# Input projection as seven block products in place of eight, in two passes over half of k

## The chip, the core and the metric

The program runs on one core of a Trainium2 chip. The metric is the device time of one execution in microseconds. All times of single instructions below come from one profiled execution of the kernel.

## What is computed

One decoder layer with two gated branches. Cut to what the change touches:

```python
h, gate = modulate(xp, c_prompt, g_norm[l], w_ada[l], b_ada[l])      # (tokens, 2048)
(q_a, k_a, v_a, z_a, q_b, k_b, v_b, z_b, q_i, k_i, w_i, g_a, g_b) = jnp.split(h @ w_in, offs, axis=-1)
q_a = rope(q_a.reshape(B, T, N_QH_A, HEAD_DIM), pos)                # k_a, q_b, k_b, q_i, k_i alike
...
s = jnp.einsum('bthd,bsd->bths', q_i, k_i) * (IDX_DIM ** -0.5)      # index scores
scores = jnp.einsum('bths,bth->bts', jax.nn.relu(s), w_i)           # then the top 256 keys of a row
...
y = (sigmoid(g_a) * u_a + sigmoid(g_b) * u_b) @ w_out
```

All is in float32. There are 1024 prompt tokens and 64 sample tokens, 1088 columns in all, and 10052 columns of w_in.

## The kernel before

The kernel is written engine by engine, in raw instructions with semaphores; each engine runs its own list in the order in which it is written, and no planner moves anything. TensorE multiplies float32 as three products of rounded parts: w_hi x h_hi, w_hi x h_lo and w_lo x h_hi, where the remainder ("lo") is the raw value less its rounded part ("hi").

Activations stand transposed: h_hi and h_lo hold 16 k tiles of 128 rows by 1088 tokens. The projection goes through w_in in tiles of 128 columns. Three index tiles come first (first_products, third_products; leave_index turns them by the rotary angle on VectorE), then the index scores (index_scores on VectorE, relu on ScalarE), then 76 main tiles in products (N_MAIN 44 and N_GATE 32, the last two in last_products). For a main tile SP loads w_raw, 1 MB (load_tile), ScalarE rounds it (split_hi), VectorE subtracts (split_lo), and TensorE runs three token chunks (CHUNKS, 384, 352 and 352 columns), each 16 k x 3 matmuls into a bank of PSUM. A finished chunk leaves its bank through ScalarE with its activation function (leave_act) or, for q and k, through VectorE with the rotary turn (leave_rotated: swapped halves times the sine into rot_b, values times the cosine into rot_a, the sum into col). GpSimd does no arithmetic in this stretch; it issues the stores of col to the scratch array proj. The table RUNS says which tiles leave how, and in which of them VectorE does rounds of the top 8 search (pick_round: MAX8 and MATCH_REPLACE8 on a row of 1088 scores, eight rounds a tile in 28 tiles).

While tiles of the gate columns run, conditioned and folded put in the matmuls of the adaLN gate (16 groups). After the last tile the attention begins (pe_attention and its likes): it loads keys and values back from proj into k_t and v_t, over the memory of h_hi and h_lo.

Main lines: matmuls L293 to L295, split_hi L279, split_lo L284, leave_act L372, leave_rotated L388 to L403, index scores L2258 to L2269, top 8 L2216 and L2218, h_lo L2544, the later weights' remainder u_lo L1944, GpSimd's o_raw L1836 and L1839.

## Time and profile before

| | us |
|---|---|
| median of 3 runs | 3147.2 |
| lowest, highest | 3143.88, 3154.12 |
| span of the profiled execution, first to last instruction | 3146.0 |
| of it: projection of the 76 main tiles | 1823.1 |
| of it: attention, merge and output | 1107.3 |

The profile has TensorE's matmuls (PE) and weight loads (PEld), VectorE (DVE), ScalarE (ACT), GpSimd (POOL) and SP's DMA issues (SPq). "Busy" is the time in which an engine executes. A matmul's time is longer than the distance to the next one, since they overlap; the distance between starts is what counts. "Idle before" names what an engine waited for.

### The profile page before, as it was taken

How to read it: one execution, taken by the hardware profiler on the slowest of the kernel's cores; microseconds unless marked ns; L12 is line 12 of the kernel's file. 1: busy time of each engine (PE TensorE's matmuls, PEld its weight loads, DVE VectorE, ACT ScalarE, POOL GpSimd, SP SyncE). 2: the span in 40 equal slices, each digit the busy share in tenths (PEclk: the TensorE clock that was granted, in tenths of full speed). 3: DMA queues.
4: the chain of work that ended last, by engine and by line, in shares of the span. 5: the costliest groups of instructions: out<-in, count | busy, mean ns of one | idle time of the engine just before them, and what ended most of it. 6: DMA issues, size and time to landing. Idle time of an engine off the chain costs nothing. (4 is left out here: it accounts for less than half of the span.)

```text
span 3146.0 us, 50501 instructions
## 1 busy us (share of the span) xinstructions
PE 3054.7 (97%) x19803; PEld 2881.1 (92%) x19811; DVE 1693.4 (54%) x2463; ACT 749.9 (24%) x1173; POOL 266.7 (8%) x516
## 2 busy tenths in 40 slices
PE   5989999999999999999999999999999999999998
PEld 4869999999999999999999999988876897998986
DVE  4573786200786355555455554566654544654755
ACT  5240000011000111211111111165433323333333
POOL 3100000000000000000000000042224101010000
PEclk8999999999999999999999999999999999999999
DMA  9832222222222222333233232565269774683672
GB/s 350 282 114 70 75 74 61 82 61 61 82 75 61 94 63 75 105 93 102 75 95 109 81 102 75 181 198 147 85 188 312 215 269 158 194 269 127 207 237 98
DMA packets 452309, 425.08 MB, mean 135 GB/s; under 512 B 20628, under 2 KB 393620, under 8 KB 449108
## 3 DMA queue, kind: packets, MB, share of 16 engines
q1 hardware_dynamic: 428998, 343.06, 36.8%
q0 software_dynamic: 22048, 78.45, 6.7%
q10 hardware_dynamic: 1152, 2.13, 0.2%
q8 instruction: 65, 1.06, 0.1%
q14 instruction: 46, 0.38, 0.0%
HBM read 348.79 MB, written 76.88 MB: 135 GB/s over the span
## 5 line engine op out<-in xcount | busy, mean ns | idle before, releaser
L293 PE MATMUL banks<-h_hi,w_hi 128*128 128x352 f32 (+1 forms) x3552 | 1162.5, 327 | 0.0
L295 PE MATMUL banks<-h_hi,w_lo 128*128 128x352 f32 (+1 forms) x3552 | 1158.3, 326 | 0.0
L294 PE MATMUL banks<-h_lo,w_hi 128*128 128x352 f32 (+1 forms) x3552 | 1157.4, 326 | 0.0
L293 PEld LDWEIGHTS banks<-h_hi,w_hi 128*128 128x128 f32 x3552 | 666.8, 188 | 3.1 <-issue 3.0
L294 PEld LDWEIGHTS banks<-h_lo,w_hi 128*128 128x128 f32 x3552 | 669.2, 188 | 0.0
L295 PEld LDWEIGHTS banks<-h_hi,w_lo 128*128 128x128 f32 x3552 | 666.2, 188 | 0.0
L284 DVE TENSOR_TENSOR w_lo<-w_raw,w_hi 128x2048 fp32r<-128x2048 f32 x77 | 175.4, 2278 | 657.3 <-ACT w_hi L279 519.6
L372 ACT ACTIVATE col<-banks 128x384 f32<-128x384 f32 x150 | 71.2, 474 | 1023.6 <-PE banks L295 984.0
L1944 DVE TENSOR_TENSOR u_lo<-u_raw,u_hi 128x1536 fp32r<-128x1536 f32 (+1 forms) x96 | 196.4, 2046 | 200.4 <-ACT u_hi L1858 200.0
L2216 DVE MAX8 best<-work 128x8 f32<-128x1088 f32 x224 | 289.1, 1291 | 10.0
L2218 DVE MATCH_REPLACE8 work<-best,work 128x1088 f32<-128x1088 f32 x224 | 285.9, 1276 | 0.0
L279 ACT CAST w_hi<-w_raw 128x2048 fp32r<-128x2048 f32 x77 | 146.0, 1896 | 570.7 <-PE banks L295 552.8
L1858 ACT CAST u_hi<-u_raw 128x1536 fp32r<-128x1536 f32 (+1 forms) x96 | 162.8, 1696 | 410.8 <-PE banks L2202 231.1
L2200 PE MATMUL banks<-u_hi,m_hi 128*128 128x512 f32 x512 | 200.0, 391 | 5.8 <-DVE u_lo L1944 5.8
L2201 PE MATMUL banks<-u_hi,m_lo 128*128 128x512 f32 x512 | 199.7, 390 | 0.0
L2202 PE MATMUL banks<-u_lo,m_hi 128*128 128x512 f32 x512 | 199.7, 390 | 0.0
L2136 PE MATMUL banks<-o_hi,u_hi 128*128 128x384 f32 (+1 forms) x576 | 188.1, 327 | 1.0 <-DVE u_lo L1944 0.9
L2386 POOL DMA_DIRECT2D scratch_proj<-col x76 | 40.4, 531 | 1749.5 <-ACT col L372 1125.6
L2138 PE MATMUL banks<-o_hi,u_lo 128*128 128x384 f32 (+1 forms) x576 | 187.7, 326 | 0.0
L2137 PE MATMUL banks<-o_lo,u_hi 128*128 128x384 f32 (+1 forms) x576 | 187.6, 326 | 0.0
L388 DVE TENSOR_TENSOR rot_b<-banks,rot_sin 64x384 f32<-64x384 f32 (+1 forms) x156 | 83.2, 533 | 176.5 <-PE banks L295 174.6
L2200 PEld LDWEIGHTS banks<-u_hi,m_hi 128*128 128x128 f32 x512 | 96.5, 188 | 26.2 <-DVE u_lo L1944 6.2
(313 smaller groups left out, 3432.0 us busy)
## 6 DMA issues: line engine op xcount, KB each, us to landing
w_raw<-in_w_in SPq DMA_DIRECT2D x76, 1024.0 KB, 5.5
u_raw<-in_w_out SPq DMA_DIRECT2D x96, 512.0 KB, 5.0
scratch_proj<-col POOLq DMA_DIRECT2D x76, 544.0 KB, 3.0
ada_w<-in_w_ada SPq DMA_DIRECT2D x16, 2048.0 KB, 13.9
u_raw<-in_w_pb SPq DMA_DIRECT2D x48, 512.0 KB, 4.9
...
```

The costliest lines, as they stand in the source:

```text
L293: nc.tensor.matmul(dst, w_hi[:, par, k, 0:width], h_hi[:, k, a:b], start=(k == 0), stop=False)
L294: nc.tensor.matmul(dst, w_hi[:, par, k, 0:width], h_lo[:, k, a:b], start=False, stop=False)
L295: mm = nc.tensor.matmul(dst, w_lo[:, par, k, 0:width], h_hi[:, k, a:b], start=False, stop=(k == KT - 1))
L1944: nc.vector.tensor_tensor(u_lo[u % 2][:, 0:ks, :], u_raw[:, u, 0:ks, :], u_hi[u % 2][:, 0:ks, :], ALU.subtract).then_inc(u_lo_set, 1)
L2136: nc.tensor.matmul(dst, u_hi[par][:, k, :], hi[:, k, 0:n], start=(k == (whole or ks)[0]), stop=False)
L2137: nc.tensor.matmul(dst, u_hi[par][:, k, :], lo[:, k, 0:n], start=False, stop=False)
L2138: mm = nc.tensor.matmul(dst, u_lo[par][:, k, :], hi[:, k, 0:n], start=False, stop=(k == (whole or ks)[-1]))
L2200: nc.tensor.matmul(dst, high, hi[:, x, :], start=first, stop=False)
L2201: nc.tensor.matmul(dst, low, hi[:, x, :], start=False, stop=False)
L2202: mm = nc.tensor.matmul(dst, high, lo[:, x, :], start=False, stop=last)
L2216: nc.vector.max(best8[:], work[:])
L2218: nc.vector.match_replace(work[:], best8[:], work[:], TAKEN)
```

## The change

The 76 main tiles become 38 pairs, and each pair a product of 2 by 2 blocks: tokens in two halves of HT = 544 columns, a pair's two tiles, and k in two sets. Seven block products (P1 to P7, Strassen's form in Winograd's order) take the place of eight. They need sums of blocks on either side. On the side of h these are S1 to S4, made once for a pass; on the side of the weights four sums a step (t1 to t4, weight_sums on GpSimd). Each of the seven weight blocks is split into hi (ScalarE) and lo (VectorE five, GpSimd two). Since h, its sums and all hi and lo parts don't fit at once, the whole runs in two passes over half of k: steps 0 to 37 with k tiles 0 to 7, steps 38 to 75 with k tiles 8 to 15. In the first pass the half sums are stored to proj; in the second they are loaded into col (part_landed) and the products of the second half added. k tiles 8 to 15 of h are stored to DRAM by SP while they are made, combined by GpSimd in steps 2 to 17 (prepared), and loaded again around step 38.

A product is 2 pieces x 4 k x 3 matmuls of PC = 272 columns. Results leave the banks by additions on VectorE (add_bank) and, in steps that don't turn, by copies on ScalarE (act_out_of; in the second pass to snap, which GpSimd adds to col). In the 13 steps with q and k ("turned"; four of them, "class", with columns ordered by class) the rotary turn works on whole quarters of col, after the sums: swapped on VectorE (two multiplications of 64 partitions x 544 with the sine, from SBUF), by_cosine on GpSimd, turned on VectorE. SP issues the stores that GpSimd issued. Top 8 rounds are four a step in 32 steps of the first pass and 4 or 5 a step in 21 of the second. Steps are written out on all engines but TensorE, which loops over two at a time.

The order of TensorE in a step s is P1, P4 of step s-1, P2, P6, P5, P7, P3. P6 waits for p1_out, P7 for u2_out and P3 for p5_out: additions or copies of what P1, P6 and P5 left.

```diff
+HT, PC = TOK // 2, TOK // 4
+KB = KT // 4
+PAIRS = (N_MAIN + N_GATE) // 2
+STEPS = 2 * PAIRS
...
+        SECOND_PASS = list(KINDS)
+        pair_of = lambda s: s if s < PAIRS else SECOND_PASS[s - PAIRS]
+        kind_of = lambda s: "half" if s < PAIRS else KINDS[SECOND_PASS[s - PAIRS]]
+        turns = lambda s: kind_of(s) in ("turned", "class")
+        direct = lambda s: turns(s) or s > 0 and turns(s - 1)
+        snaps = lambda s: s >= PAIRS and not direct(s)
+        LAST = STEPS - 1
...
+        PICK_ROUNDS = {}
+        for x in range(4):
+            for s in range(2 + 9 * x, 10 + 9 * x):
+                PICK_ROUNDS[s] = (x, 4)
+        PICK_LATE = SNAP_STEPS[0] + 1
+        for x in range(3):
+            for y in range(7):
+                PICK_ROUNDS[PICK_LATE + 7 * x + y] = (4 + x, 5 - y % 2)
...
-            sp.wait_ge(ada_used, 14)
-            load_tile(sp, 2, *IDX_SRC[2])
-            sp.dma_start(rot_cos[:], ins["rot"][2]).then_inc(rot_ready, 16)
-            sp.dma_start(rot_sin[:], ins["rot"][3]).then_inc(rot_ready, 16)
+            for k in range(KT // 2, KT):
+                sp.wait_ge(lo_set, k + 1)
+                for x, rows in enumerate((h_hi, h_lo)):
+                    sp.dma_start(scr["merged"][x * KT // 2 + k - KT // 2], rows[:, k, :].bitcast(F32)).then_inc(h_saved, 16)
+                if k == KT - 3:
+                    sp.wait_ge(ada_used, 14)
+                    load_index_last()
...
+        def weight_sums(pool, s):
+            par = s % 2
+            t1, t2, t3, t4 = (hole(xn_t, HOLE[c]) for c in (3, 2, 4, 6))
+            b11, b12, b21, b22 = (part_of(par, x) for x in ("B11", "B12", "B21", "B22"))
+            pool.wait_ge(raw_landed[par], 16 * (s // 2 + 1))
+            need(pool, lo_dve, 5 * s)
+            need(pool, lo_pool, 2 * s)
+            nc.gpsimd.tensor_tensor(t3, b22, b12, ALU.subtract).then_inc(t_set, 1)
+            pool.wait_ge(t_set, 4 * s + 1)
+            nc.gpsimd.tensor_tensor(t2, t3, b11, ALU.add).then_inc(t_set, 1)
+            if turns(s - 1):
+                by_cosine(pool, s - 1, 0)
+            nc.gpsimd.tensor_tensor(t1, b12, b11, ALU.subtract).then_inc(t_set, 1)
+            pool.wait_ge(t_set, 4 * s + 2)
+            nc.gpsimd.tensor_tensor(t4, b21, t2, ALU.subtract).then_inc(t_set, 1)
...
+        def by_cosine(pool, s, place):
+            x = TURN_ORDER[place]
+            dst = col[s % 2][:, int(x[1]) - 1, FIRST if x[0] == "1" else SECOND]
+            pool.wait_ge(swap_set, turn_no(s, place))
+            pool.wait_ge(rot_ready, 64)
+            nc.gpsimd.tensor_tensor(dst, dst, rot_cos[:, FIRST if x[0] == "1" else SECOND], ALU.mult).then_inc(cos_set, 1)
...
+        def low_weights(pool, s, c):
+            pool.wait_ge(wc_hi_set, HI_NO[s, c])
+            src = part_of(s % 2, "B22") if c == 5 else hole(xn_t, HOLE[c])
+            nc.gpsimd.tensor_tensor(wc_lo[c][:], src, wc_hi(c), ALU.subtract).then_inc(lo_pool, 1)
...
+        def pool_step(pool, s):
+            low_weights(pool, s, 5)
+            if s and turns(s - 1):
+                by_cosine(pool, s - 1, 2)
+            if snaps(s):
+                add_snap(pool, s, 0)
+            low_weights(pool, s, 6)
+            if s and turns(s - 1):
+                by_cosine(pool, s - 1, 3)
+            if s + 1 < STEPS:
+                weight_sums(pool, s + 1)
+            if snaps(s):
+                add_snap(pool, s, 1)
+                add_snap(pool, s, 2)
+            if turns(s):
+                by_cosine(pool, s, 1)
...
+            pool.wait_ge(third_half, 3)
+            pool.wait_ge(h_saved, 16 * KT)
+            s3, s1, s2, s4 = (hblock(xn_t, name) for name in ("S3", "S1", "S2", "S4"))
+            nc.gpsimd.tensor_tensor(s1, plain(h_hi, "A21"), plain(h_lo, "A21"), ALU.add).then_inc(s_set, 1)
+            nc.gpsimd.tensor_tensor(s3, plain(h_hi, "A11"), plain(h_lo, "A11"), ALU.add).then_inc(s_set, 1)
+            pool.wait_ge(s_set, S_NO["x3"])
+            nc.gpsimd.tensor_tensor(s3, s3, s1, ALU.subtract).then_inc(s_set, 1)
+            nc.gpsimd.tensor_tensor(s2, plain(h_hi, "A22"), plain(h_lo, "A22"), ALU.add).then_inc(s_set, 1)
+            nc.gpsimd.tensor_tensor(s4, plain(h_hi, "A12"), plain(h_lo, "A12"), ALU.add).then_inc(s_set, 1)
+            pool.wait_ge(s_set, S_NO["x4"])
+            nc.gpsimd.tensor_tensor(s4, s4, s2, ALU.subtract).then_inc(s_set, 1)
+            nc.gpsimd.tensor_tensor(s1, s1, s2, ALU.add).then_inc(s_set, 1)
+            pool.wait_ge(s_set, S_NO["S1"])
+            nc.gpsimd.tensor_tensor(s2, s2, s3, ALU.subtract).then_inc(s_set, 1)
+            weight_sums(pool, 0)
+            nc.gpsimd.tensor_tensor(s4, s4, s3, ALU.add).then_inc(s_set, 1)
+            for s in range(STEPS):
+                pool_step(pool, s)
...
+        def low_weights_dve(dve, s, c):
+            dve.wait_ge(wc_hi_set, HI_NO[s, c])
+            src = hole(xn_t, HOLE[c]) if c in HOLE else part_of(s % 2, {0: "B11", 1: "B21"}[c])
+            nc.vector.tensor_tensor(wc_lo[c][:], src, wc_hi(c), ALU.subtract).then_inc(lo_dve, 1)
+        def low_block(dve, n):
+            name = X_ORDER[n]
+            dve.wait_ge(x_hi_set, n + 1)
+            if n < 4:
+                dve.wait_ge(s_set, S_NO["S4" if name == "S3" else name])
+            nc.vector.tensor_tensor(hblock(h_lo, name), hblock(xn_t, name), hblock(h_hi, name), ALU.subtract)\
+                .then_inc(x_lo_set, 1)
+        def add_bank(dve, s, x, bank, place, out):
...
+            dve.wait_ge(p_done, done(s, place))
+            if s >= PAIRS:
+                dve.wait_ge(part_landed[s % 2][q], 16 * sum(y % 2 == s % 2 for y in range(PAIRS, s + 1)))
...
+            dst = of_col(s % 2, x)
+            nc.vector.tensor_tensor(dst, pair_bank(bank), dst, ALU.add).then_inc(out, 1)
+        def swapped(dve, s, place):
+            x = TURN_ORDER[place]
+            dve.wait_ge((c11_out, c22_out, c12_out, c21_out)[place], s + 1)
...
+            cols = FIRST if x[0] == "1" else SECOND
+            src = col[s % 2][:, int(x[1]) - 1, cols]
+            half = HD // 2
+            for q in (0, half):
+                last = nc.vector.tensor_tensor(turn_b[half - q:P - q, :], src[q:q + half, :], rot_sin[q:q + half, cols],
+                                               ALU.mult)
+            last.then_inc(swap_set, 1)
+        def turned(dve, s, place):
+            x = TURN_ORDER[place]
+            dve.wait_ge(cos_set, turn_no(s, place))
+            cols = FIRST if x[0] == "1" else SECOND
+            src = col[s % 2][:, int(x[1]) - 1, cols]
+            dve.wait_ge(swap_set, turn_no(s, place))
+            if kind_of(s) != "class":
+                nc.vector.tensor_tensor(src, src, turn_b[:], ALU.add).then_inc(turned_set, 1)
+                return
...
+        def dve_step(dve, s):
+            par, more, rot = s % 2, s + 1 < STEPS, turns(s)
+            was = s and turns(s - 1)
+            if s:
+                add_bank(dve, s - 1, "12", BANK_D, "P3", c12_out)
+            if s == PAIRS:
+                low_block(dve, 7)
+            if was:
+                turned(dve, s - 1, 1)
+                swapped(dve, s - 1, 2)
+            if direct(s):
+                add_bank(dve, s, "11", BANK_A(par), "P1", p1_out)
+            if more:
+                low_weights_dve(dve, s + 1, 0)
+            rounds(dve, s, 0)
+            if was:
+                turned(dve, s - 1, 2)
+            if s > PAIRS:
+                add_bank(dve, s - 1, "21", BANK_A(1 - par), "P4", c21_out)
+            if was:
+                swapped(dve, s - 1, 3)
+            if s == PAIRS:
+                low_block(dve, 8)
+            add_bank(dve, s, "11", BANK_B, "P2", c11_out)
+            if was:
+                turned(dve, s - 1, 3)
+            if rot:
+                swapped(dve, s, 0)
+            if more:
+                low_weights_dve(dve, s + 1, 1)
...
+            if s == PAIRS:
+                low_block(dve, 9)
...
+            rounds(dve, s, 1)
+            if direct(s):
+                add_bank(dve, s, "12", BANK_A(par), "P6", u2_out)
+            if rot:
+                turned(dve, s, 0)
+            if more:
+                low_weights_dve(dve, s + 1, 2)
...
+            rounds(dve, s, 2)
+            if s == PAIRS:
+                low_block(dve, 10)
+            if direct(s):
+                add_bank(dve, s, "22", BANK_D, "P5", p5_out)
+            if more:
+                low_weights_dve(dve, s + 1, 3)
+            add_bank(dve, s, "22", BANK_A(par), "P7", c22_out)
...
+            if rot:
+                swapped(dve, s, 1)
+            if more:
+                low_weights_dve(dve, s + 1, 4)
...
+            rounds(dve, s, 3)
...
+        def product(pe, x, bank, fresh):
+            c, name = {"P1": (0, "A11"), "P2": (1, "A12"), "P6": (2, "S2"), "P5": (3, "S1"), "P7": (4, "S3"),
+                       "P3": (5, "S4"), "P4": (6, "A22")}[x]
+            hi, lo = wc_hi(c), wc_lo[c]
+            for piece in range(2):
+                dst = banks[:, bank + piece, 0:PC]
+                for j in range(KB):
+                    high, low = moving(h_hi, name, j, piece), moving(h_lo, name, j, piece)
+                    nc.tensor.matmul(dst, hi[:, j, :], high, start=(fresh and j == 0), stop=False, skip_group_check=True)
+                    nc.tensor.matmul(dst, hi[:, j, :], low, start=False, stop=False, skip_group_check=True)
+                    mm = nc.tensor.matmul(dst, lo[:, j, :], high, start=False, stop=(j == KB - 1), skip_group_check=True)
+            mm.then_inc(p_done, 1)
...
+        def step(pe, s, par, x_waits=(0,) * 7, scores=0, gate=None, fold=None):
...
+            product(pe, "P1", BANK_A(par), True)
+            if not first:
+                fourth(pe, s - 1, 1 - par, x_waits[6])
+            pe.wait_ge(lo_dve, 5 * s + 2)
...
+            need(pe, c11_out, s)
+            product(pe, "P2", BANK_B, True)
+            pe.wait_ge(lo_dve, 5 * s + 3)
+            need(pe, x_lo_set, x_waits[2])
+            pe.wait_ge(p1_out, s + 1)
+            product(pe, "P6", BANK_A(par), False)
+            pe.wait_ge(lo_dve, 5 * s + 4)
...
+            need(pe, c12_out, s)
+            product(pe, "P5", BANK_D, True)
+            pe.wait_ge(lo_dve, 5 * s + 5)
...
+            pe.wait_ge(u2_out, s + 1)
+            product(pe, "P7", BANK_A(par), False)
...
+            pe.wait_ge(lo_pool, 2 * s + 1)
...
+            pe.wait_ge(p5_out, s + 1)
+            product(pe, "P3", BANK_D, False)
```

On TensorE, at a change of chunk of a main tile before (the first three rows are the last of a chunk of 384 columns):

```order
L293 MATMUL banks<-h_hi,w_hi 128x384
L294 MATMUL banks<-h_lo,w_hi 128x384
L295 MATMUL banks<-h_hi,w_lo 128x384
L293 MATMUL banks<-h_hi,w_hi 128x352
L294 MATMUL banks<-h_lo,w_hi 128x352
L295 MATMUL banks<-h_hi,w_lo 128x352
```

and now, at the change from P1 to P2 in step 0 (wc_hi0 and wc_lo0 are the parts of weight block 0):

```order
L3116 MATMUL banks<-h_hi_59,wc_hi0_69 128x272
L3117 MATMUL banks<-h_lo_60,wc_hi0_69 128x272
L3118 MATMUL banks<-h_hi_59,wc_lo0_72 128x272
L3116 MATMUL banks<-h_hi_59,wc_hi1_70 128x272
L3117 MATMUL banks<-h_lo_60,wc_hi1_70 128x272
L3118 MATMUL banks<-h_hi_59,wc_lo1_73 128x272
```

The pattern of three is kept; a group has 12 matmuls of 272 columns where it had 48 of 352 or 384.

On GpSimd, behind the last operation of the index, before (ki_two is the index key, acc the scores):

```order
L2360 DMA scratch_proj<-ki_two_90 64x1088
L2363 DMA scratch_score<-acc0_82 128x1088
L2363 DMA scratch_score<-acc1_83 128x1088
L2363 DMA scratch_score<-acc0_82 128x1088
L2363 DMA scratch_score<-acc1_83 128x1088
```

and now (xn_t is the memory of h_lo; raw0 the raw weights of step 0):

```order
L2652 TENSOR_TENSOR xn_t_61<-h_hi_59,h_lo_60 128x4x544
L2653 TENSOR_TENSOR xn_t_61<-h_hi_59,h_lo_60 128x4x544
L2655 TENSOR_TENSOR xn_t_61<-xn_t_61 128x4x544
L2656 TENSOR_TENSOR xn_t_61<-h_hi_59,h_lo_60 128x4x544
L2657 TENSOR_TENSOR xn_t_61<-h_hi_59,h_lo_60 128x4x544
L2659 TENSOR_TENSOR xn_t_61<-xn_t_61 128x4x544
L2660 TENSOR_TENSOR xn_t_61<-xn_t_61 128x4x544
L2662 TENSOR_TENSOR xn_t_61<-xn_t_61 128x4x544
L2548 TENSOR_TENSOR xn_t_61<-raw0_79 128x4x128
L2550 TENSOR_TENSOR xn_t_61<-xn_t_61,raw0_79 128x4x128
L2553 TENSOR_TENSOR xn_t_61<-raw0_79 128x4x128
L2555 TENSOR_TENSOR xn_t_61<-raw0_79,xn_t_61 128x4x128
```

The stores of the scores went to SP, and arithmetic stands on GpSimd at that place.

On VectorE, a chunk and a half of a turned tile before:

```order
L388 TENSOR_TENSOR rot_b_69<-banks,rot_sin_66 64x384 x2
L390 TENSOR_TENSOR rot_a_68<-banks,rot_cos_65 128x384
L403 TENSOR_TENSOR col_67<-rot_a_68,rot_b_69 128x384
L126 REGISTER_ALU
L382 REGISTER_ALU
L388 TENSOR_TENSOR rot_b_69<-banks,rot_sin_66 64x352 x2
L390 TENSOR_TENSOR rot_a_68<-banks,rot_cos_65 128x352
```

and now, about half of the first class step (col0 and col1 are the columns of even and odd steps, turn_b the swapped quarter):

```order
L2880 TENSOR_TENSOR col1_82<-banks,col1_82 128x544
L2893 TENSOR_TENSOR turn_b_84<-col1_82,rot_sin_95 64x544 x2
L2880 TENSOR_TENSOR col0_81<-banks,col0_81 128x544
L2905 TENSOR_TENSOR col1_82<-col1_82,turn_b_84 128x544
L2893 TENSOR_TENSOR turn_b_84<-col0_81,rot_sin_95 64x544 x2
L2854 TENSOR_TENSOR wc_lo1_73<-raw1_80,wc_hi1_70 128x512
L2880 TENSOR_TENSOR col0_81<-banks,col0_81 128x544
L2909 TENSOR_TENSOR turn_o_85<-col0_81,turn_b_84 128x136x4
L2854 TENSOR_TENSOR wc_lo2_74<-xn_t_61,h_hi_59 128x512
L2880 TENSOR_TENSOR col0_81<-banks,col0_81 128x544
```

The multiplications with the sine read SBUF where they read a bank, and the cosine has gone to GpSimd:

```order
L2576 TENSOR_TENSOR wc_lo5_77<-raw1_80,wc_hi5_71 128x512
L2563 TENSOR_TENSOR col0_81<-col0_81,rot_cos_94 128x544
L2576 TENSOR_TENSOR wc_lo6_78<-xn_t_61,h_hi_59 128x512
L2563 TENSOR_TENSOR col0_81<-col0_81,rot_cos_94 128x544
L2548 TENSOR_TENSOR xn_t_61<-raw0_79 128x4x128
L2550 TENSOR_TENSOR xn_t_61<-xn_t_61,raw0_79 128x4x128
L2563 TENSOR_TENSOR col1_82<-col1_82,rot_cos_94 128x544
L2553 TENSOR_TENSOR xn_t_61<-raw0_79 128x4x128
L2555 TENSOR_TENSOR xn_t_61<-raw0_79,xn_t_61 128x4x128
L2563 TENSOR_TENSOR col1_82<-col1_82,rot_cos_94 128x544
```

That is GpSimd's list of one turned step; before it had no arithmetic there.

## Rows read from the trace of the kernel before

**Rows 1.** The page, part 1: busy time and share of the span.
```profile
PE 3054.7 (97%) x19803; PEld 2881.1 (92%) x19811; DVE 1693.4 (54%) x2463; ACT 749.9 (24%) x1173; POOL 266.7 (8%) x516
```

**Rows 2.** Windows by stage: length, each engine's busy time, granted clock, DMA share, GB/s.
```profile
0.00:77.00 77.00, 41.90 (x375) 33.12 (x375) 31.34 (x55) 39.16 (x56) 25.98 (x54) 0.87 1.02 349
...
181.90:215.60 33.70, 26.75 (x177) 9.63 (x177) 28.90 (x40) 23.07 (x28) 3.53 (x6) 0.95 0.35 128
215.60:2038.70 1823.10, 1823.10 (x11489) 1816.42 (x11490) 941.28 (x1088) 229.11 (x253) 47.30 (x89) 1.00 0.28 85
```

**Rows 3.** Timeline of VectorE, 600 to 650: start, duration, instruction, idle before.
```profile
620.79 2.29 DVE L284 TENSOR_TENSOR w_lo<-w_raw,w_hi 128x2048 fp32r<-128x2048 f32 x1 [21.62 <-ACT w_hi L279]
644.53 2.29 DVE L284 TENSOR_TENSOR w_lo<-w_raw,w_hi 128x2048 fp32r<-128x2048 f32 x1 [21.45 <-ACT w_hi L279]
```

**Rows 4.** Timeline of TensorE: first and last of 20 matmuls, and of 3 with 256 columns.
```profile
1100.86 0.32 PE L293 MATMUL banks<-h_hi,w_hi 128*128 128x352 f32 x1
...
1103.92 0.32 PE L294 MATMUL banks<-h_lo,w_hi 128*128 128x352 f32 x1
...
2207.44 0.28 PE L1112 MATMUL banks<-k_hi,q_hi 128*128 128x256 f32 x1
...
2207.68 0.29 PE L1114 MATMUL banks<-k_hi,q_lo 128*128 128x256 f32 x1
```

**Rows 5.** Groups of VectorE by line and form: busy us, mean ns, idle before.
```profile
L2216 DVE MAX8 best<-work 128x8 f32<-128x1088 f32 x224 | 289.1, 1291 | 10.0
L2218 DVE MATCH_REPLACE8 work<-best,work 128x1088 f32<-128x1088 f32 x224 | 285.9, 1276 | 0.0
L284 DVE TENSOR_TENSOR w_lo<-w_raw,w_hi 128x2048 fp32r<-128x2048 f32 x76 | 174.1, 2291 | 652.2 <-ACT w_hi L279 514.5 <-DMA work<-scratch_score 133.5 <-issue 3.1
L2004 DVE TENSOR_TENSOR y_row<-banks,y_row 128x512 f32<-128x512 f32 x32 | 22.1, 692 | 1.1
...
L2544 DVE TENSOR_TENSOR h_lo<-xn_t,h_hi 128x1088 fp32r<-128x1088 f32 x16 | 20.0, 1288 | 8.4 <-ACT h_hi L2422 8.4
```

**Rows 6.** Groups of GpSimd and ScalarE by line and form.
```profile
L872 POOL TENSOR_TENSOR k_lo<-k_t,k_hi 128x512 fp32r<-128x512 f32 x4 | 5.1, 1266 | 0.0
...
L1836 POOL TENSOR_TENSOR o_raw<-o_s,z_raw 128x768 f32<-128x768 f32 x1 | 1.8, 1841 | 79.9 <-DMA z_raw<-scratch_proj 79.9
...
L779 ACT CAST k_hi<-k_t 128x512 fp32r<-128x512 f32 x4 | 2.4, 607 | 0.0
```

**Rows 7.** Timelines of GpSimd and VectorE, 2598 to 2613 and 2818 to 2838.
```profile
2820.39 1.84 POOL L1836 TENSOR_TENSOR o_raw<-o_s,z_raw 128x768 f32<-128x768 f32 x1 [79.91 <-DMA z_raw<-scratch_proj]
...
2820.43 3.96 DVE L1944 TENSOR_TENSOR u_lo<-u_raw,u_hi 128x2048 fp32r<-128x2048 f32 x1 [5.87 <-ACT u_hi L1858]
...
2600.03 2.38 DVE L1944 TENSOR_TENSOR u_lo<-u_raw,u_hi 128x2048 fp32r<-128x2048 f32 x1 [15.34 <-ACT u_hi L1858]
...
2600.21 3.07 POOL L1839 TENSOR_TENSOR o_raw<-o_raw,z_raw 128x384 f32<-128x384 f32 x1
...
2603.24 1.01 POOL L1839 TENSOR_TENSOR o_raw<-o_raw,z_raw 128x384 f32<-128x384 f32 x1
2603.67 0.69 DVE L1992 TENSOR_TENSOR banks<-banks,gate_p 128x512 f32<-128x512 f32 x1
```

**Rows 8.** Timeline of VectorE: the index's last operation, a score operation.
```profile
180.20 0.52 DVE L348 TENSOR_TENSOR ki_two<-rot_a,rot_b 64x352 f32<-64x352 f32 x1
...
191.47 0.89 DVE L2261 SCALAR_TENSOR_TENSOR acc<-relu_s,wi_tok,acc 128x640 f32<-128x640 f32 x1
```

**Rows 9.** Timelines of SP and VectorE: third index tile, h_lo of k 12, first leave_index.
```profile
126.84 2.25 SPq L267 DMA_DIRECT2D w_raw<-in_w_in  x1
...
133.64 2.49 DVE L2544 TENSOR_TENSOR h_lo<-xn_t,h_hi 128x1088 fp32r<-128x1088 f32 x2 [0.78 <-ACT h_hi L2422]
...
150.97 2.25 DVE L340 TENSOR_TENSOR rot_b<-banks,rot_sin 32x384 f32<-32x384 f32 x4
```

**Rows 10.** Timeline of TensorE behind the last tile: the first class product.
```profile
2048.75 0.71 PE L1066 MATMUL banks<-k_class,q_class 128*128 128x128 f32 x4
```

1011 lines of the change are left out of this document (661 added, 350 removed).

## Prediction

> **What bounds the kernel now.** I read the page's engine shares first, then the windows by stage, the groups by line, and the timelines. TensorE is busy for 97% of the 3146.0 us span [rows 1]. In the window of the input projection, 215.6 to 2038.7, it is busy for all 1823.10 us at the full granted clock, while VectorE has work for 941.28 us, ScalarE for 229.11 and GpSimd for 47.30 [rows 2]. So only fewer or shorter matmuls help there, and the other three engines have room. The stage before it is another case: scores of the index, 33.7 us, VectorE busy for 28.90 and TensorE for 26.75 [rows 2]. VectorE sets its pace.
>
> **The price of a matmul.** One tile of 128 columns goes from one w_lo to the next in 644.53 - 620.79 = 23.74 us [rows 3], for 144 matmuls of 384 or 352 columns. 76 tiles are 1804.2 us. With 352 columns the starts lie (1103.92 - 1100.86)/19 = 161 ns apart, with 256 columns (2207.68 - 2207.44)/2 = 120 ns [rows 4]. Both are the columns at 2.4 GHz (147, 107) plus 13 to 14 ns. For 272 columns that gives 113.3 + 13.2 = 126.5 ns. The bounds are 125 (a straight line between the two rows) and 131 (if loading the weights, once for each matmul, begins to count); I go by the nearest row, 256 columns.
>
> **Products: -189 us.** New are 76 steps (38 pairs of tiles, two halves of k) with 7 products x 2 pieces x 4 k x 3 = 168 matmuls, so 12768 in place of 10944, but 7/8 of the columns. 12768 x 126.5 ns = 1615 us against 1804 us; a step is 21.25 us, a product 3.04. The 16 gate matmul groups stay.
>
> **First pass, 38 steps: 0.** Cover is the 21.25 us of TensorE. VectorE has five remainders of 512 (w_lo of 2048 took 2291 ns, h_lo of 1088 took 1288, so 1.04 ns an element and 0.16: 0.69 us [rows 5]), three additions from a bank of 544 (512 took 692 ns [rows 5], so 0.72), and in 32 steps four rounds of the top 8 at 1.291 + 1.276 + 0.09 [rows 5]: 3.5 + 2.2 + 10.6 = 16.3 us. GpSimd has six operations on 512 at 1.27 us [rows 6], 7.6 us. ScalarE has seven casts at 0.61 us [rows 6] and three copies, 6 us. Each product's weights have the six other products to be made, 18 us. All fits, with 5 us to spare on VectorE; what ran over would show as TensorE's gap.
>
> **The queue that is missed: VectorE against GpSimd.** [rows 7] show it. At 2820.39 GpSimd starts an operation of 1.84 us, at 2820.43 VectorE a subtraction of two SBUF operands that otherwise takes 2.29 us: it takes 3.96, so it stood until GpSimd was done. At 2600.21 a GpSimd operation of about 1 us takes 3.07, since VectorE's subtraction of 2600.03 runs until 2602.41. But VectorE's multiplication with a PSUM operand at 2603.67 has 0.69 us with GpSimd at work from 2603.24. So two SBUF operands on VectorE and any GpSimd operation exclude each other, wait whole, and take turns; additions from banks don't.
>
> The Trainium skill ("SBUF — State Buffer", section on SBUF's two separate sides) states this as an exclusive lock for VectorE operations with two SBUF inputs or in a 2-port mode, against a GpSimd operation, held for the whole instruction. The trace agrees for the first kind; no row shows the second. By the page MAX8, with one input, stays free of it; were that wrong, the sum would be that of the slow rival below.
>
> **Start of the projection: +42 us for the scores, +5.5 behind them.** Behind rot_set 9 GpSimd's queue now holds eight operations on 2176 elements, four on 512 and one more on 2176. 768 took 1.84 us, 512 took 1.27 [rows 6]: 2.1 ns an element, so 2176 takes 4.75 us. VectorE's score operations read relu_s and acc, both SBUF, and take 0.3 to 1.35 us. Taking turns, each waits for one whole GpSimd operation: 9 x 4.65 + 4 x 1.15 = 46.4 us of lock, with 13 of VectorE's 35 score operations in between. rot_set 9 comes with the last index operation, at 180.7 [rows 8] and now 188.2. With GpSimd's DMA issue of 0.6 and 6.6 us of VectorE in between, the chain is over at 241.8, with VectorE done with the second operation of the 640-wide tile; before it was there at 192.4 [rows 8]. 241.8 - (192.4 + 7.5) = 42 us later. Bounds: 0 (no exclusion for these forms) and 46. I take 42, since two of the operands are as in [rows 7]. TensorE then waits 2.5 us in step 0 for the split of the four sums, and comes from a stretch with little work: in the first 77 us, at 54% busy, the granted clock was 0.87 on average [rows 2], so 3 us more for a first product at 1.2 GHz.
>
> **Third index tile and its rotary tables: +7.5 us.** On SP's queue they were issued from 126.84, and VectorE began to leave the index at 150.97 [rows 9]. Now 12 stores of 0.56 MB stand ahead of them, of which the last two wait for h_lo of k 13, whose pair starts at 133.64 [rows 9]. At the 349 GB/s of the first window [rows 2] the ada_w loads end at about 134 (an estimate: what follows them was issued at 126.84, and one load of 2.1 MB takes 6 us at that rate); 6.7 MB more at 0.36 MB/us are 18.5 us: to 152.5; then the tile with 272-byte rows, 3 us, and two tables of 0.56 MB, 3 us: 158.5. So +7.5 us, from +6 to +9. It is on the path, since VectorE then works through to the scores without a gap.
>
> **Turned steps of the second pass: +45 us.** These are 13 steps (q and k; four by class). VectorE: seven additions from banks 5.0, five remainders 3.5, eight half-height multiplications on two SBUF operands 5.8, four additions of two SBUF operands 2.9 (strided by class about 1.2 each, 4.8). GpSimd: 6 x 1.27 + 4 cosines of 544 at 1.33 = 12.9. Locked time, less 0.12 us at each start: GpSimd 11.5, VectorE 10.0 (11.9 by class); 21.5 and 23.4 us, already more than 21.25. And the order is a chain: swapped, cosine, turned for each quarter. Followed row by row, with turns taken, u2_out (VectorE, queued behind swapped and the remainder of B21) comes 16.5 us after the step's start where P7 could start at 15.2, and p5_out at 21.2 where P3 could start at 19.5. P3 ends at 24.3, by class at 26.3. 9 x 3.05 + 4 x 5 = 47, less one counted below: 45. Bounds 20 (locked time alone decides) and 75.
>
> **Change of pass: +7 us.** Four remainders of 2176 at 2.4 us fall on VectorE in step 38, 20.7 us of its own and about 9 of GpSimd's lock: 6 us over, 1 in step 37. **Other steps of the second pass: 0.** VectorE has four additions, five remainders and 4.6 rounds, 18.6 us, and waits some 1.6 us for GpSimd's 11.6: 20.2, just under 21.25.
>
> **End: +4 us.** The last half of k_t and v_t, 3.3 MB, is loaded only after P7; before, the class products began at 2048.75, 10 us after the last product [rows 10]. 3.3 MB at 0.38 MB/us is 9 us from 3 us ahead of the end, and the q_class loads come behind.
>
> **Sum.** -189 + 42 + 5.5 + 7.5 + 45 + 7 + 4 = -78 us. The profiled span was 3146.0 us, the median of the three runs 3147.2, 1.2 more: 3147.2 - 78 = 3069 us.
>
> **Rivals.** (a) The exclusion hides: score operations don't collide, or GpSimd is shorter. Without the 42 the start of TensorE waits 6.5 in place of 5.5 us for the sums: 3028; with half of the turned term off also, 3005; with all off, 2983. For it: rows 7 show one form only. Against: the operands are alike. (b) Slower than before: the top 8 rounds collide with GpSimd too. A step of the second pass's end then has 18.6 us of VectorE and most of GpSimd's 10.4 locked us in series, about 26.7, +5.5 x 21; in the first pass the eight steps with five or more long GpSimd operations go over by 7: +56. 115 + 56 = 171: 3240. It is slower than now once such a step takes over 25 us. Against: no second SBUF tensor streams in MAX8. (c) The turned steps are at 75 and the matmul at 129 ns: 3069 + 30 + 32 = 3131. (d) The change doesn't take work away: if the start of a matmul were bound by the weight load at 141 ns, 12768 of them would equal the old 1804 and the rest would make 3258; the 256-column row is against it.
>
> **Chances.** The forecast 0.46 (3040 to 3100), (a) 0.24, (b) 0.10, (c) 0.13, (d) 0.03, near no change 0.04. Range: 3000 to 3135 leaves out the all-hidden end of (a), (b) and (d). Faster by over 0.3%, which is about what a measurement can tell: 0.46 + 0.24 + 0.11 = 0.81; within 0.05; slower 0.14.
>
> **What would show it.** Score operations on VectorE of 4 to 5 us each and GpSimd's nine long ones from 189 to 242; matmuls of 272 columns 126 to 127 ns apart; first-pass steps of 21.3 us without a gap on TensorE; turned steps of 24 to 26 us with TensorE waiting for additions from banks ahead of P7 and P3. Wrong would be: score operations at their old lengths, or gaps in the steps with top 8 rounds.

## The result: 1.4% slower

The changed kernel takes 3192.4 us (median of 4, 3189.2 to 3194.1), the kernel before 3147.3. The ratio is 1.0139, interval 1.0125 to 1.0153. The forecast was 3069 us, with a range of 3000 to 3135. The profiled execution has a span of 3192.6 us, 46.6 more than the 3146.0 of before. The runs below whose time stands without a number of runs were each measured once.

The page's first part after the change, against [rows 1]:

```profile
PE 2918.5 (91%) x21635; PEld 2728.3 (85%) x21635; DVE 2176.8 (68%) x2948; ACT 1030.2 (32%) x1748; POOL 1171.8 (37%) x1096
```

TensorE has 136 us less work than before and the kernel is still longer: the share fell from 97 to 91%. The windows by stage show where (columns as in [rows 2]). The stages are: up to the scores; scores; steps 0 to 36; 37 and 38 (change of pass); 39 to 50 (turned); 51 to 53; 54 to 75; the rest.

```profile
0.00:188.60 188.60, 145.25 (x1201) 120.81 (x1202) 99.19 (x180) 65.62 (x98) 36.21 (x73) 0.94 0.95 317
188.60:264.00 75.40, 32.24 (x195) 12.22 (x193) 68.56 (x42) 23.19 (x31) 50.65 (x14) 0.68 0.17 62
264.00:1074.00 810.00, 803.62 (x6742) 798.91 (x6735) 594.51 (x714) 250.20 (x430) 390.55 (x310) 1.00 0.47 149
1074.00:1140.00 66.00, 47.23 (x338) 46.65 (x337) 41.57 (x36) 24.30 (x26) 22.49 (x14) 0.84 0.67 227
1140.00:1449.00 309.00, 270.77 (x2018) 266.34 (x2017) 279.19 (x296) 52.17 (x84) 183.03 (x120) 0.96 0.40 128
1449.00:1513.00 64.00, 63.55 (x506) 63.36 (x505) 41.84 (x44) 16.13 (x27) 38.55 (x27) 1.00 0.52 163
1513.00:2073.00 560.00, 492.94 (x3726) 484.08 (x3725) 428.85 (x484) 166.12 (x259) 270.42 (x194) 0.96 0.40 135
```

In the first pass TensorE is busy for 803.6 of 810 us. Before it the score stage takes twice its time, and in the second pass TensorE is without matmuls for 38 us in the turned steps and for 67 in the last 22.

Counted from the matmuls of 272 columns (168 a step), whose starts give each step's length:

| term | forecast, us | measured, us |
|---|---|---|
| matmuls, 76 steps of 21.11 us in place of 76 tiles of 23.74 | -189 | -200 |
| first matmul of the projection at 264.05, before at 215.6 (scores 42, index tile 7.5) | +49.5 | +48.5 |
| step 0 (27.9 us for its six products) | +5.5 | +9.8 |
| steps 1 to 36, beyond the gate matmuls that before had too | 0 | +3.4 |
| change of pass, steps 37 and 38 (36.4 and 29.7 us) | +7 | +23.9 |
| steps 39 to 50 (25.0, by class 27.3 us) and 51 | +45 | +56.5 |
| steps 52 to 75 | 0 | +92.2 |
| behind the last product (1119.4 us, before 1107.3) | +4 | +12.1 |
| sum | -78 | +46.4 |

One line holds more than half of the error of 123 us: the last steps of the second pass, forecast at 21.1 us each. From step 55 on a step lasts 23.2 to 23.7 us where VectorE runs four top 8 rounds in that time and 25.2 to 26.0 where it runs five, and 27 and 34 us at each of the two changes to a new row. VectorE works about half a step late, so the steps of 26 us are those behind a step that has five rounds in the table PICK_ROUNDS.

### The profile page after: what moved, and what is told of

It is laid out like the page before. It is cut to its first block and busy times, and to the rows that moved or that the text cites. A ratio compares the mean times of both kernels' runs of the same rounds, so it can differ in the third digit from the quotient of the medians.

```text
span 3192.6 us, 56880 instructions
## 1 busy us (share of the span) xinstructions
PE 2918.5 (91%) x21635; PEld 2728.3 (85%) x21635; DVE 2176.8 (68%) x2948; ACT 1030.2 (32%) x1748; POOL 1171.8 (37%) x1096
## 5 line engine op out<-in xcount | busy, mean ns | idle before, releaser
L3118 PE MATMUL banks<-h_hi,wc_lo 128*128 128x272 f32 x4256 | 1242.0, 292 | 0.0
L3116 PE MATMUL banks<-h_hi 128*128 128x272 f32 x2432 | 720.3, 296 | 107.5 <-DVE col L2880 58.4
L3118 PEld LDWEIGHTS banks<-h_hi,wc_lo 128*128 128x128 f32 x4256 | 816.2, 192 | 0.0
L3117 PE MATMUL banks<-h_lo,h_hi 128*128 128x272 f32 x2432 | 714.8, 294 | 0.0
L3116 PEld LDWEIGHTS banks<-h_hi 128*128 128x128 f32 x2432 | 471.8, 194 | 119.5 <-issue 57.4
L3116 PE MATMUL banks<-h_hi,wc_hi 128*128 128x272 f32 x1824 | 530.4, 291 | 23.4 <-ACT col L2700 15.2
L3117 PE MATMUL banks<-h_lo,wc_hi 128*128 128x272 f32 x1824 | 528.1, 290 | 0.0
L3117 PEld LDWEIGHTS banks<-h_lo,h_hi 128*128 128x128 f32 x2432 | 472.5, 194 | 0.0
L3116 PEld LDWEIGHTS banks<-h_hi,wc_hi 128*128 128x128 f32 x1824 | 345.5, 189 | 29.8 <-issue 29.0
L3117 PEld LDWEIGHTS banks<-h_lo,wc_hi 128*128 128x128 f32 x1824 | 345.8, 190 | 0.0
L2880 DVE TENSOR_TENSOR col<-banks,col 128x544 f32<-128x544 f32 x309 | 220.8, 720 | 135.4 <-PE banks L3118 126.2
L2303 DVE MATCH_REPLACE8 work<-best,work 128x1088 f32<-128x1088 f32 x224 | 285.9, 1276 | 0.6 <-issue 0.6
```

Of the source, the lines that this page charges most:

```text
L2303: nc.vector.match_replace(work[:], best8[:], work[:], TAKEN)
L2880: nc.vector.tensor_tensor(dst, pair_bank(bank), dst, ALU.add).then_inc(out, 1)
L3116: nc.tensor.matmul(dst, hi[:, j, :], high, start=(fresh and j == 0), stop=False, skip_group_check=True)
L3117: nc.tensor.matmul(dst, hi[:, j, :], low, start=False, stop=False, skip_group_check=True)
L3118: mm = nc.tensor.matmul(dst, lo[:, j, :], high, start=False, stop=(j == KB - 1), skip_group_check=True)
```

## The scores: two engines that take turns

GpSimd and VectorE in the score stage of the changed kernel, from their timelines (start, duration, instruction):

```profile
189.42 4.79 POOL L2652 TENSOR_TENSOR xn_t<-h_hi,h_lo 128x2176 f32<-128x2176 f32 x1
...
191.39 7.75 DVE L2344 TENSOR_SCALAR acc<-relu_s,wi_tok 128x384 f32<-128x384 f32 x1 [0.60 <-ACT relu_s L2841]
199.27 14.99 DVE L2347 SCALAR_TENSOR_TENSOR acc<-relu_s,wi_tok,acc 128x384 f32<-128x384 f32 x3
...
234.83 5.01 POOL L2664 TENSOR_TENSOR xn_t<-xn_t 128x2176 f32<-128x2176 f32 x1
```

Three operations of 384 columns take 15 us. Without GpSimd beside them they take 2.1 (below). GpSimd's chain ends at 239.84, and was put at 241.8. The operation at 191.39 (L2344) reads one tensor only, relu_s, and a column of scalars, and it waits too: 7.75 us, where it takes 0.42 us without GpSimd. But it could still be that GpSimd's traffic of any kind slows VectorE. So the first run gives VectorE a PSUM operand and leaves GpSimd as it is:

```diff
-                    need(act, acc_step, n - 1)
-                    nc.scalar.activation(relu_s[:, n % 2, 0:width], flat(pick_bank(n), P, width),
+                    nc.scalar.activation(flat(pick_bank(n), P, width), flat(pick_bank(n), P, width),
...
-                        nc.vector.tensor_scalar(out, relu_s[:, n % 2, 0:width], wi_tok[:, t, h:h + 1], None,
+                        nc.vector.tensor_scalar(out, flat(pick_bank(n), P, width), wi_tok[:, t, h:h + 1], None,
```

> ScalarE writes relu back into the bank it read instead of into relu_s, VectorE's score operations read it there (one PSUM operand), and TensorE waits for VectorE (acc_step) before it uses a bank again. GpSimd's nine long sums stay. Theory (VectorE with two SBUF operands and GpSimd take turns): the score operations between 189 and 240 fall from about 4 to 7.75 us back to 0.3 to 1.4, the first 272-column matmul starts some 40 us earlier, at 220 to 230 in place of 264, and the kernel takes 3192 - 40 = 3152 us; GpSimd's nine sums then end later than the scores, and the wait for them in step 0 may take a few us back. Rival (the score operations are long because GpSimd's traffic of any kind slows VectorE's reads, or because ScalarE or TensorE is late): they stay long, and the start stays at 260 or later.

Measured: 3166.3 us in place of the 3152 expected, span 3164.8. VectorE and the first matmul in that run:

```profile
192.46 0.62 DVE L2344 TENSOR_SCALAR acc<-banks,wi_tok 128x384 f32<-128x384 f32 x1 [0.58 <-ACT banks L2840]
193.20 2.07 DVE L2347 SCALAR_TENSOR_TENSOR acc<-banks,wi_tok,acc 128x384 f32<-128x384 f32 x3
195.31 4.08 DVE L2355 TENSOR_TENSOR acc<-acc,diag 128x128 f32<-128x128 f32 x1
...
219.06 4.39 DVE L2355 TENSOR_TENSOR acc<-acc,diag 128x128 f32<-128x128 f32 x1
...
240.10 0.39 PE L3115 MATMUL banks<-h_hi,wc_hi 128*128 128x272 f32 x1 [0.48 <-DVE acc L2347]
```

The same three operations now take 2.07 us in place of 14.99, and the one ahead of them 0.62 in place of 7.75, while GpSimd's sums stand beside them at 4.76 to 4.84 us each. One kind of operation among the scores had kept two SBUF operands, the addition of the diagonal mask, and it alone of them still waits: 4.08 and 4.39 us in place of 0.29. So the run shows both sides. The start moved by 24 us and not by 40. Against the next run, whose scores nothing disturbs, the additions took 9.3 us more in all, the first operations of the tiles 3.0 us more from the bank, and two remainders ahead of the last score tile 1.1 us more; some 2 us are left, with TensorE's new wait for VectorE before it uses a bank again among what can make them. The operations and their lengths came as the theory says; the start (240) missed its band of 220 to 230 by 10 us, as the additions had been overlooked, and lies far from the rival's 260.

The second run asks what the turns cost against doing one after the other:

```diff
             pool.wait_ge(h_saved, 16 * KT)
+            pool.wait_ge(acc_step, len(PICKS) * IH)
```

> Nothing is left out. GpSimd begins its nine long sums only when the last score operation is done. Theory (while both have work they take turns, so that beside one another they take no less time than one after the other): the scores end at about 223 and the first 272-column matmul starts there in place of 264; the sums then run 225 to 273, step 0 waits for them, and step 1 starts at 280 to 290, where it is 291.9 now: 0 to 10 us less in all. Rival (beside one another they do gain something, the long score operations being a small loss): step 1 starts at 300 or later, and the kernel is over 3200.

Measured: 3198.1 us, span 3196.6. From its timelines:

```profile
191.24 0.42 DVE L2344 TENSOR_SCALAR acc<-relu_s,wi_tok 128x384 f32<-128x384 f32 x1 [0.60 <-ACT relu_s L2842]
191.77 2.08 DVE L2347 SCALAR_TENSOR_TENSOR acc<-relu_s,wi_tok,acc 128x384 f32<-128x384 f32 x3
...
224.26 0.39 PE L3117 MATMUL banks<-h_hi,wc_hi 128*128 128x272 f32 x1
```

The first matmul is 39.8 us earlier, and nothing is won: step 1 starts at 296.6 in place of 291.9. Both expectations missed in part (280 to 290, and 300 or later). Step 1 starts between 291.7 and 295.6 in the changed kernel and in the four runs below that leave this stage as it is (those without activations, without late rounds, with the small cosine, and with act_ended later), so scores and sums beside one another gain some 1 to 5 us over one after the other, out of 48 us of sums. The 5.7 us on the whole kernel are one run's, and no clear difference. GpSimd's free time in this stage was hardly there to be had. The score stage was the stage that VectorE already set, as the prediction read it from [rows 2].

## The last steps: a wait in ScalarE's queue

The waits of the window 1513 to 2073 in the changed kernel: TensorE's, ScalarE's and VectorE's (us in total, times, longest):

```profile
PE banks L3116 <- ACT snap L2708: 45.8, 25, 3.7
PE banks L3116 <- DVE col L2880: 21.2, 17, 7.9
...
ACT col L2714 <- DVE col L2880: 242.4, 38, 17.1
...
DVE wc_lo L2854 <- ACT wc_hi L2680: 70.0, 40, 3.5
DVE best L2301 <- DMA work<-scratch_score: 17.9, 2, 9.0
```

TensorE waits for copies by ScalarE, ScalarE stands 242 us at L2714 for VectorE (act_ended, the silu or sigmoid on the finished columns of the step before), and VectorE waits 70 us for ScalarE's casts. No engine is busy all of the time, and two wait for each other. One turn of it, step 72, which starts at 1971.82:

```profile
1971.62 1.28 DVE L2303 MATCH_REPLACE8 work<-best,work 128x1088 f32<-128x1088 f32 x1
...
1981.44 0.72 DVE L2880 TENSOR_TENSOR col<-banks,col 128x544 f32<-128x544 f32 x1 [0.17 <-issue]
1984.42 1.43 DVE L2854 TENSOR_TENSOR wc_lo<-raw,wc_hi 128x512 fp32r<-128x512 f32 x1 [2.25 <-ACT wc_hi L2680]
...
1982.26 1.11 ACT L2714 ACTIVATE col<-col 128x1088 f32<-128x1088 f32 x1 [9.56 <-DVE col L2880]
1983.27 0.59 ACT L2708 COPY snap<-banks 128x544 f32<-128x544 f32 x1
1983.77 0.62 ACT L2680 CAST wc_hi<-raw 128x512 fp32r<-128x512 f32 x1
...
1983.92 0.40 PE L3116 MATMUL banks<-h_hi 128*128 128x272 f32 x1 [2.25 <-ACT snap L2708]
```

VectorE runs half a step behind, which harms nothing by itself: it adds P3 of step 71 to its quarter at 1981.44, behind top 8 rounds of step 71. ScalarE has act_ended of step 71 at the head of its list for step 72 and waits there for 9.56 us. Behind it in the queue stand the copy of P1, for which TensorE's P6 waits, and the cast of the next weights, for which VectorE waits 2.25 us and falls further behind. Three runs take this apart.

The activations left out:

```diff
-                KINDS[p] = kind
+                KINDS[p] = kind if isinstance(kind, str) else "plain"
```

> Silu and sigmoid of the 22 last pairs are left out, and with them act_ended, ScalarE's wait for VectorE's last additions; the columns are stored as in a plain step. Snap copies, top 8 rounds and GpSimd's additions stay. Theory A (VectorE behind its rounds, ScalarE's queue stopped in act_ended behind VectorE, and the casts that VectorE needs queued behind that): steps 55 to 75, now 25.6 us on average, fall to 22.5 with five rounds and 21.1 with four, except the two changes of row (steps 60, 61, 67, 68), 2 x 12 us over; in all 50 to 60 us less, near 3137. Theory B (VectorE's own work with the lock is the bound): five-round steps stay at 25 to 26, four-round ones at 23, and the total moves by less than 15 us.

The late rounds left out:

```diff
-            for c in range(parts[n] if n < 3 else all_ - sum(parts[0:3])):
+            for c in range((parts[n] if n < 3 else all_ - sum(parts[0:3])) if x < 4 else 0):
```

> The top 8 rounds of the last three rows (steps 53 to 73) are left out; their loads, masks and stores stay. Theories A and B both: VectorE is no longer behind, steps 55 to 75 at 21.1 to 21.5 us, about 85 us less, near 3107. Rival C (the snap copies, GpSimd's additions and the reloads of half sums make these steps long whatever VectorE does with the rest): steps stay over 22.5 us, less than 60 us in all.

The window of steps 54 to 75 in the first and in the second of these:

```profile
1508.00:2004.00 496.00, 479.56 (x3784) 479.17 (x3783) 421.17 (x491) 130.15 (x221) 269.86 (x197) 0.98 0.48 155
```

```profile
1508.00:1984.00 476.00, 474.94 (x3778) 474.56 (x3777) 204.46 (x205) 177.18 (x262) 274.79 (x197) 1.00 0.52 161
```

Without activations (3129.5 us, expected 3137) VectorE still has 421 us of work with all rounds in it, and every step is 21.11 us long, five rounds or four, except two of 31.8 and 31.1 at the changes of row. Theory B is out. Theory A was right in kind and too careful: it kept 22.5 us for five rounds. Without the late rounds (3103.4 us, expected 3107) both reasons vanish together, as both theories said; the steps are at 21.11 us but for 22.0 and 21.8 at the two changes of row. So snap copies, GpSimd's additions and reloads cost next to nothing, and rival C is out.

Then the same work with another order on ScalarE:

```diff
-            if s and curved(s - 1):
-                act_ended(act, s - 1, 1)
             if s == PAIRS:
                 high_block(act, 7)
...
             high_weights(act, s, 6)
             if s and curved(s - 1):
-                act_ended(act, s - 1, 0)
+                act_ended(act, s - 1, 1)
...
             if more:
                 high_weights(act, s + 1, 2)
+            if s and curved(s - 1):
+                act_ended(act, s - 1, 0)
```

> Nothing is left out. In ScalarE's list of a step act_ended for the tiles in quarters 12 and 22 of the step before moves from the head to a place behind the cast of block 6, and act_ended for 11 and 21 to a place behind the copy of P6 and the cast of block 2: both behind the casts and the copy that others wait for, and at times when VectorE's additions are done in a step without waits (5.8 and 10 us in, as the run without activations shows). Theory A (the wait in ScalarE's queue is the cost): steps 55 to 75 at 21.1 to 21.5 us but for the two changes of row, 35 to 45 us less, near 3150. Rival B' (the 1.1 us of ScalarE's time for each activation is the cost, so that only leaving it out helps): steps stay over 23, less than 20 us in all.

Measured: 3133.7 us, where 3150 was expected. The window of steps 54 to 75, TensorE's one line of waits in it, and two of VectorE's:

```profile
1508.00:2006.00 498.00, 477.48 (x3757) 476.87 (x3755) 419.69 (x490) 172.88 (x260) 266.54 (x195) 0.98 0.44 149
```

```profile
PE banks L3116 <- DVE col L2880: 20.1, 2, 10.5
...
DVE best L2301 <- DMA work<-scratch_score: 26.1, 2, 13.6
...
DVE wc_lo L2854 <- ACT wc_hi L2680: 8.3, 6, 1.4
```

ScalarE does as much as before (172.88 us), and the steps are at 21.11, so rival B' is out. So not the time of the activations but their place at the head of the queue was the cost: steps 52 to 75 lose 66.6 of their 92.2 us, more than the 35 to 45 expected. ScalarE's wait at act_ended falls from 242.4 us to 1.7, VectorE's wait for casts from 70.0 us in 40 places to 8.3 in 6. The kernel as a whole gains 58.7 us and not 66.6: the stage behind the last product grew by 7 us (below). What is left, 25.5 us, are two waits, one for each new row of scores: VectorE stands at MAX8 until SP has stored the mask of the old row, and loaded the new one into the same buffer, and all that VectorE has behind it waits too. The table of rounds put rows end to end there; in the first pass it leaves a step free between them.

## Turned steps

This run leaves most of GpSimd's cosine out, in its place in the list and with its waits:

```diff
-            nc.gpsimd.tensor_tensor(dst, dst, rot_cos[:, FIRST if x[0] == "1" else SECOND], ALU.mult).then_inc(cos_set, 1)
+            nc.gpsimd.tensor_tensor(dst[:, 0:8], dst[:, 0:8], rot_cos[:, 0:8], ALU.mult).then_inc(cos_set, 1)
```

> GpSimd's multiplications with the cosine cover 8 columns in place of 544; order and waits stay. Theory (locked time of both engines and the chain of swapped, cosine, turned set the turned steps): steps 39 to 50, now 25.0 plain and 27.3 by class, lose most of four times 1.2 us, to 21.1 to 22 and 22.5 to 24, in all 40 us less, near 3153. Rival (VectorE's own queue is the bound there): less than 1.5 us a step, under 18 us in all.

Measured: 3156.6 us. The window of steps 39 to 50 and TensorE's waits in it, against the 309.00 us of the changed kernel above:

```profile
1140.00:1413.00 273.00, 261.29 (x2036) 256.71 (x2035) 262.49 (x299) 52.80 (x85) 135.97 (x122) 1.00 0.45 145
```

```profile
PE banks L3116 <- DVE col L2880: 11.7, 24, 1.1
```

The steps fall from 25.0 and 27.3 to 22.2 and 23.2 us, 38 us in the stage and 36 in all, near the 40 that the theory (locked time and the chain of swapped, cosine and turned) gives; the rival had under 18. The run doesn't tell the chain from the locked time, since the small cosine shortens both. TensorE's waits in the changed kernel's stage are 38.1 us in 20 places; the 11.7 that are left were not taken apart.

## Both ends of the second pass

At the change of pass the changed kernel shows, on ScalarE and in SP's queue:

```profile
1102.41 2.00 ACT L2689 CAST h_hi<-xn_t 128x2176 fp32r<-128x2176 f32 x1 [13.88 <-DMA xn_t<-scratch_resid]
...
1094.67 16.73 SPq L2403 DMA_DIRECT2D xn_t<-scratch_resid  x5
```

The block for P2 could be loaded from 1083.3 on, when P2 of step 37 was done. SP issued it at 1094.67, behind two stores of step 36 and two loads of half sums that wait for them. ScalarE's cast of it stood ahead of the copy of P5, and P3 waited 12.5 us for that copy.

All of this went into one kernel, in stages that don't overlap. The main parts that were not shown yet follow, shortened. The mask in the first score operation and the place of a row's first rounds at the end of a step are as the expectation says:

```diff
+            sp.wait_ge(ada_used, 14)
+            load_index_last()
             for k in range(KT // 2, KT):
...
-                PICK_ROUNDS[PICK_LATE + 7 * x + y] = (4 + x, 5 - y % 2)
+                PICK_ROUNDS[PICK_LATE + 7 * x + y] = (4 + x, 5 if y else 2)
...
+                if s == PAIRS - 1:
+                    for n in ((5,), (6, 7))[1 - q]:
+                        load_block(sp, n)
...
-            if s == PAIRS - 1:
-                high_block(act, 5)
             if not direct(s):
                 act_out_of(act, s, "22", BANK_D, "P5", p5_out)
+            if s == PAIRS - 1:
+                high_block(act, 5)
```

> Nothing is left out. Six edits in stages that don't overlap: relu in the bank (24 us by the run with the scores there); the diagonal mask as in1 of the first score operation of the last 128 columns, from a bank, in place of an addition of two SBUF operands (8 us); the third index tile and its tables issued ahead of the 16 stores of h (7.5 us, to the time of the kernel before); act_ended later (40 us); a row's seven steps with 2, 5, 5, 5, 5, 5, 5 rounds, the first two at the end of the step, when the row has landed (20 us); at the change of pass two of SP's blocks of h issued between the stores of step 36, and the cast of the second block behind the copy of P5 (10 us). By theory A and the taking of turns the sum is 110 us: 3083 us, 2.0% under the kernel before. Rival: the gaps move to the next one that waits (VectorE's total with the lock in five-round steps, the loads at the change of pass), and half is lost: 3135.

Measured: 3068.7 us (4 runs, 3064.6 to 3072.7), ratio to the kernel before 0.9749, interval 0.9733 to 0.9765. That is 14 us less than the 3083 expected, for act_ended and the new table bring 87 us together where 60 were counted. The first matmul starts at 228.8 (35 us earlier), steps 52 to 75 are 4.9 us over, steps 37 and 38 together 15.8 in place of 23.9: step 37 is at 21.11, but step 38 grew from 29.7 to 36.9. There the rival was right in part: the gap moved one step on. TensorE's waits are 9.7 us of that step's excess; the rest is matmuls at a lower clock (0.82 on average).

One stage got worse. Behind the last product the changed kernel, and then this one, show for the first class product and the loads that it waits for:

```profile
2093.55 1.20 PE L1151 MATMUL banks<-k_class,q_class 128*128 128x128 f32 x4 [7.48 <-DMA q_class<-scratch_proj]
...
2075.28 1.30 SPq L2374 DMA_DIRECT2D scratch_proj<-col  x2
2076.62 39.52 SPq L718 DMA_DIRECT2D q_class<-scratch_proj  x16
```

```profile
1966.77 1.19 PE L1151 MATMUL banks<-k_class,q_class 128*128 128x128 f32 x4 [7.43 <-DMA q_class<-scratch_proj]
...
1946.67 1.65 SPq L2375 DMA_DIRECT2D scratch_proj<-col  x2
1948.37 40.43 SPq L718 DMA_DIRECT2D q_class<-scratch_proj  x16
```

From the last product (2073.2, 1939.6) it is 20.4 us and 27.2 us; before it was 10.1 [rows 10]. With act_ended later alone it is 27.0 us already, so that edit made the stage worse. The reading is that stores ahead of the loads in SP's queue wait for ScalarE, which now does act_ended later. So the last run moves both back:

```diff
-            for q in (1, 0):
-                store_col(sp, LAST, q)
             sp.wait_ge(class_out, 16 * CLASS_STORES)
             load_class(0)
+            for q in (1, 0):
+                store_col(sp, LAST, q)
...
+            if s == LAST:
+                act_ended(act, s - 1, 0)
```

> The kernel with the six edits, and two more at the end: act_ended for quarters 11 and 21 of step 74 stands in step 75 directly behind the one for 12 and 22, and SP issues the 16 loads of q_class ahead of the two stores of the last pair. Before these, TensorE's first class product starts 27.2 us after the last 272-column matmul (20.4 in the changed kernel, 10.1 in the kernel before), because the last loads wait in SP's queue behind stores that wait for ScalarE. Theory (SP's order of issue is the cost there): it starts 17 to 20 us after, and the kernel takes 7 to 10 us less, 3060. Rival (the loads themselves, 3.3 MB of keys and values and then the class queries, are the cost): it stays at 25 or more, within 3 us of 3068.

```profile
1959.93 1.19 PE L1151 MATMUL banks<-k_class,q_class 128*128 128x128 f32 x4 [5.04 <-DMA q_class<-scratch_proj]
...
1942.62 12.21 SPq L718 DMA_DIRECT2D q_class<-scratch_proj  x8
```

It starts 17.3 us after the last product (1942.6), within the 17 to 20 expected; the two moves were made together, and their shares stay open. The kernel takes 3061.3 us (4 runs, 3057.6 to 3062.4), ratio 0.9717, interval 0.9698 to 0.9736: 88 us under the kernel before in the same job. The change is worth having once its queues are put in order.

## The prediction, point by point

**Price of a matmul: right, 0.8 ns high.** Two matmuls of the first product, 39 starts apart:

```profile
265.16 0.29 PE L3118 MATMUL banks<-h_hi,wc_lo 128*128 128x272 f32 x1
...
270.08 0.29 PE L3118 MATMUL banks<-h_hi,wc_lo 128*128 128x272 f32 x1
```

4.92 / 39 = 126.2 ns, and over the step 21.11 / 168 = 125.7, between the low bound of 125 and the 126.5 taken. Rival (d), a start bound by the weight load, is out. That is 11 us better than forecast.

**Scores and index tile: right, in part by luck.** 48.5 against 49.5: the index ends at 188.5 (forecast 188.2), and the turns taken with GpSimd do the rest. Rival (a) is out. The luck lies in one premise. The prediction had all score operations read two SBUF tensors, but the first of each tile reads one. These first operations waited as well, 12 of the 40.6 us by which VectorE's operations are longer here than in the run with the sums behind the scores; had they stayed free, the term would have been too large. The prediction's two rows for GpSimd give 2.2 ns an element and not the 2.1 taken, so 5.0 us for 2176; 4.76 to 5.08 were measured.

Rival (b) is out as well, as a mechanism: in the window 1513 to 2073 the rounds have kept their length beside GpSimd, and the remainders have not (VectorE's groups there):

```profile
L2303 DVE MATCH_REPLACE8 work<-best,work 128x1088 f32<-128x1088 f32 x94 | 120.0, 1276 | 0.3 <-issue 0.3
L2301 DVE MAX8 best<-work 128x8 f32<-128x1088 f32 x93 | 119.5, 1285 | 19.0 <-DMA work<-scratch_score 17.9
...
L2854 DVE TENSOR_TENSOR wc_lo<-raw,wc_hi 128x512 fp32r<-128x512 f32 x42 | 62.9, 1497 | 70.0 <-ACT wc_hi L2680 70.0
```

MAX8 has 1285 ns against 1291 in [rows 5], MATCH_REPLACE8 1276 against 1276, whereas a remainder of 0.69 us free takes 1.50. The Trainium skill's page "SBUF — State Buffer", section on the two separate sides, says both: an operation of VectorE with two SBUF inputs contends with GpSimd, and one with at most one, outside the modes that use two ports, doesn't. The trace agrees, with these numbers.

**Other steps of the second pass, 0: the step that failed.** The sum for VectorE (20.2 us in 21.25) held: with all rounds and all activations the steps are at 21.11 us once the order is changed. What it left out is that a sum of busy times bounds a step only if nobody waits in a queue for somebody who is late. VectorE's lateness is harmless until a queue with urgent work behind it waits for it, and ScalarE's did. The prediction looked in this way only at the turned steps, row by row; for the last 22 steps it stopped at the sum. It also saw neither the activations as waits (ScalarE was counted by its time only, and only in the first pass) nor the reload of `work` between two rows. The first made 66.6 of the 92.2 us, as moving act_ended shows; the two changes of row made the other 25.5, of which the kernel with six edits keeps 4.9. TensorE stands idle for 67 of the 92 us; most of the rest, some 18 us, is matmuls that start further apart behind such waits, mainly at half the clock, and stood in no term of these steps.

One sign of being wrong that the prediction named did show, gaps in steps with top 8 rounds, but for another reason than it gave: steps 55 to 74 last 25.7 us on average, and rival (b) had 26.7 with rounds that collide with GpSimd. That closeness is chance.

**Turned steps: right in kind, a little low.** 25.0 against 24.3, by class 27.3 against 26.3; 56.5 against 45 us in all. The method that was used here, both engines row by row with turns taken, is the one that the last steps lacked.

**Step 0: 9.8 against 5.5,** not taken apart. **Change of pass: the term is three times too small.** 7 us were VectorE's surplus in step 38. The late issue of the blocks on SP's queue, and ScalarE's cast ahead of the copy of P5, were not in it. How step 38's remaining 15.8 us divide between loads and VectorE's four long remainders stays open.

**End: 12.1 against 4.** 3.3 MB behind the last product was in the sum, the order on SP was not: 9.9 us of the 27.2 in the kernel with six edits went with two lines moved. The 17.3 that remain, against 10.1 before, were not taken apart.

**Rival (c)** (turned steps at 75, matmul at 129 ns) is out: the steps were at 56.5 and the matmul at 125.7 ns. The slower outcome came by a mechanism that stood in no rival.
